# RWKV's triangular inverse: 32x32 block transposes on VectorE in place of the second update product on TensorE

## The chip, the cores and the metric

The kernel runs on one core of a Trainium2 chip. A core has five engines with a queue each: TensorE (PE, matmuls from SBUF into PSUM), VectorE (DVE), ScalarE (ACT), GpSimd (POOL) and SyncE (SP, which issues DMAs here). They meet through semaphores alone: an instruction that has to wait for a count holds everything behind it on its own engine. The metric is the device time of one execution in microseconds (us); lower is better.

## The reference

One inference step of a hybrid layer: sparse attention beside an RWKV-7 time mixing, then a gated sum, an output projection and an MLP. The change concerns the time mixing, whose recurrence is written step by step:

```python
def rwkv7_mix(p_rw, shift0, wkv0, p):
    ...
    def step(S, inp):
        r_t, d_t, k_t, v_t, kk_t, b_t = inp
        sa = jnp.einsum('bhij,bhj->bhi', S, kk_t)
        S = (S * d_t[:, :, None, :] - sa[..., None] * b_t[:, :, None, :]
             + v_t[..., None] * k_t[:, :, None, :])
        return S, jnp.einsum('bhij,bhj->bhi', S, r_t)

    S_T, ys = lax.scan(step, wkv0.astype(f32),
                       (tm(r_h), tm(decay), tm(k_h), tm(v_h), tm(kk), tm(b_h)))
```

There are 8 heads of 64 channels, a prompt of 512 tokens and 8 samples of 16 tokens.

## The kernel before

The 640 tokens are five tiles of 128, and each tile is two chunks of 64 tokens. The order is the samples' tile first (`TILE_AT`, tile 0 of the stage), then the four of the prompt. Inside a chunk the recurrence is solved at once: the products of the decayed keys give a strictly triangular 64x64 matrix per head, and the inverse of the identity minus it is needed. It is built by doubling. The 2x2 blocks are known directly, and each of the levels 0, 1, 2, ... merges neighbouring blocks to size 4, 8, 16, 32, 64 (`merges(i)`: 3 levels for the samples, whose chunks are 16 long, 5 for the prompt; level 4 is written out apart). So before the last level the matrix is block-diagonal with blocks of at most 32x32.

`invs[i % 2]` holds, for two groups of four heads (p = 0 and 1; the two chunks lie in the lower and upper 64 partitions), the inverse (index 0) and its transpose (index 1). One level is a ring through three engines, once for each p:

- `pe_part` (L999): 8 matmuls, the level's masked block matrix times the inverse, into PSUM;
- `act_part` (L1681): ScalarE copies the product to `part`;
- `pe_update`: 16 matmuls, alternately L1019 (transposed inverse and `part`, the update of the inverse) and L1021 (`part` and the transposed inverse, the update of its transpose); a tile's last level has L1021 alone;
- `dve_inverse` (L2228): VectorE adds both updates to `invs[:, p]` in one instruction of 128x512.

An fp32 matmul of this kind is two records in the trace, so 8 matmuls show as x16. The masked matrices (`merge`, L722) come from GpSimd.

The head of a tile: `pe_pairs` (L956) makes two sets of key products. VectorE masks the first into `br` (L2203), takes the 2x2 blocks from it (`dve_first`, L2210 and L2213, which give the transposed first level), for p = 0 and p = 1 in turn, and then masks the second set into `kr` (L2203 again). `pe_first` (L976) transposes the first level with the identity, 8 matmuls for each p, and `act_first` (L1672) copies the result to `invs[:, p, 0]`. Level 0's `pe_part` waits for that copy, for `kr` and for the mask.

The order on each engine is written out by hand. Tile 0 is prepared alone; then `pe_from_v(0)` (L939, a helper's line: small products of several kinds), the pairs of tile 1 and its levels, mixed with the samples' states; then a loop over i = 1, 2, 3, in which tile i's state steps (`pe_from_state`, `pe_u` L1058, `pe_to_state`, `pe_u_to_state`, `pe_outputs`, most of them L939; VectorE's `dve_state`, L2234 and L2236, after them) are set between the first levels of tile i + 1; then tile 4 alone. In the loop `pe_from_state(i, 1, 0)` follows `pe_first` and waits for the first `dve_state`, which stands behind `kr` in VectorE's queue. `pe_turn` (L967) transposes three operands of a tile on TensorE. After the stage come the attention steps, the branch products and the MLP, all dense.

Of the kernel before, what the change touches and what calls it, by code (L numbers as in the profile page):

```python
# [246 lines left out]
def merges(i):  # L247

    return 5 if i else 3
# [10 lines left out]


def g_sets(i):

    return 2 * i - 1 if i else 0
# [45 lines left out]
def build(nc, dram):  # L310
# [130 lines left out]
    with ExitStack() as ctx:  # L441
        def sem(name):
            return ctx.enter_context(nc.semaphore(name))
# [36 lines left out]
        pair_mm, pair_set, merge_set = [sem("pair_mm0"), sem("pair_mm1")], sem("pair_set"), sem("merge_set")  # L480
        inv_t_first, first_turned, inv_first = sem("inv_t_first"), sem("first_turned"), sem("inv_first")
        part_mm, part_set, update_mm, inv_set = sem("part_mm"), sem("part_set"), sem("update_mm"), sem("inv_set")
# [289 lines left out]
        def _(pe):  # L772
# [151 lines left out]
            def half(n):  # L924

                return slice(HD * n, HD * n + HD)
# [42 lines left out]

            def pe_first(i):  # L970

                for p in range(2):
                    pe.wait_ge(inv_t_first, 2 * i + p + 1)
                    for j in range(4):
                        for c in range(2):
                            done = mm(acc[half(c), p, 512 + j * HD:512 + (j + 1) * HD], invs[i % 2][half(c), p, 1, j, :],  # L976
                                      ident[half(c), half(c)], start=True, stop=True)
                    done.then_inc(first_turned, 1)

            def pe_part(i, level, p):  # L980
# [22 lines left out]
            def pe_update(i, level, p):  # L1003

                n, last = stage(i, level), level == merges(i) - 1
                pe.wait_ge(part_set, 2 * n + p + 1)
                inv, inv_t = invs[i % 2][:, p, 0], invs[i % 2][:, p, 1]
                if level == 4:
                    for j in range(4):
                        for c in range(2):  # L1010
                            at_ = 768 + j * HD + HB
                            done = mm(acc[first(c), p, at_:at_ + HB], part[second(c), 4 * p + j, 0:HB], inv_t[second(c), j, HB:HD],
                                      start=True, stop=True)
                    done.then_inc(update_mm, 1)
                    return
                for j in range(4):
                    for c in range(2):
                        if not last:
                            mm(acc[half(c), p, 512 + j * HD:512 + (j + 1) * HD], inv_t[half(c), j, :], part[half(c), 4 * p + j, :],  # L1019
                               start=True, stop=True)  # L1020
                        done = mm(acc[half(c), p, 768 + j * HD:768 + (j + 1) * HD], part[half(c), 4 * p + j, :],  # L1021
                                  inv_t[half(c), j, :], start=True, stop=True)
                done.then_inc(update_mm, 1)
# [111 lines left out]
            pe_turn(0, 0)  # L1135
            pe_first(0)
            for level in range(merges(0)):
# [28 lines left out]
            done.then_inc(u_mm, 1)  # L1166
            pe_first(1)
            pe.wait_ge(u_set, 1)
# [20 lines left out]
            for i in range(1, NT - 1):  # L1189
# [14 lines left out]
                pe_turn(following, 0)  # L1204
                pe_first(following)
                pe_from_state(i, 1, 0)
# [258 lines left out]
        def _(act):  # L1465
# [202 lines left out]

            def act_first(i):
                for p in range(2):  # L1670
                    act.wait_ge(first_turned, 2 * i + p + 1)
                    do(A(columns(invs[i % 2][:, p, 0]), acc[:, p, 512:768], ACT.Copy), inv_first)  # L1672

            def act_part(i, level):
# [34 lines left out]
            act_turned(0, 0)  # L1709
            act_first(0)  # L1710
            act_part(0, 0)
# [12 lines left out]
            act_u(0, every)  # L1724
            act_first(1)
            act_turned(1, 0)
# [11 lines left out]
            for i in range(1, NT - 1):  # L1738
# [3 lines left out]
                act_turned(following, 0)  # L1742
                act_first(following)
                act_g(i, upper)
# [243 lines left out]
        def _(dve):  # L1988
# [209 lines left out]
            def dve_pairs(i, n, p):  # L2198
# [6 lines left out]
                   pair_set)  # L2205

            def dve_first(i, p):

                first = invs[i % 2][:, p, 1]
                do(V.tensor_tensor(first, acc[:, p, 512:1024].rearrange("q (j a d) -> q j a d", j=4, a=2)[:, :, 0, :],  # L2210
                                   over_heads(e_masks[:, E_PAIRT:E_PAIRT + HD], 4), ALU.mult))
                do.settle()
                do(V.tensor_tensor(first, first, over_heads(e_masks[:, E_IDENT:E_IDENT + HD], 4), ALU.add), inv_t_first)  # L2213

            def dve_inverse(i, level, p):

                dve.wait_ge(update_mm, 2 * stage(i, level) + p + 1)
                if level == 4:
# [4 lines left out]
                    return  # L2223
                if level == merges(i) - 1:
                    dst, src = invs[i % 2][:, p, 1].rearrange("q j d -> q (j d)"), acc[:, p, 768:1024]
                else:
                    dst, src = invs[i % 2][:, p].rearrange("q n j d -> q (n j d)"), acc[:, p, 512:1024]
                do(V.tensor_tensor(dst, dst, src, ALU.add), inv_set)  # L2228

# [416 lines left out]
```

## Time and profile before

| | us |
|---|---|
| median of 3 runs | 1146.52 (1146.48 to 1149.2) |
| the profiled execution, own time | 1146.62 |
| its span, first to last instruction | 1144.8 |
| TensorE busy | 1104.5 |
| VectorE busy | 693.5 |
| GpSimd busy | 634.3 |
| ScalarE busy | 398.5 |
| mean granted clock of TensorE | 0.990 |

Busy time is the time in which an engine had an instruction under way; idle time of an engine that nobody waits for costs nothing. Times inside the trace are counted from the span's start. The granted clock is a share of TensorE's full 2.4 GHz.

### The profile page before, as it was taken

The numbers are of one execution on the slowest core, as the hardware profiler recorded it, in microseconds if no ns is written. First come the engines' busy times: TensorE is split into PE (matmuls) and PEld (weight loads), VectorE is DVE, ScalarE is ACT, GpSimd is POOL, SyncE is SP. The second block draws the span as 40 slices with busy tenths as digits, with TensorE's granted clock in tenths as the row PEclk, the third lists the DMA queues.
The fourth block names the chain that finished last, engine by engine and source line by source line (L and its number), as shares of the span: only waits on it lengthen the run. The fifth ranks groups of instructions, "written<-read, shape, count | busy, mean of one in ns | idle before, by whom it ended". The sixth has DMA issues, their size and how long they took to land.

```text
span 1144.8 us, 25249 instructions
## 1 busy us (share of the span) xinstructions
PE 1104.5 (96%) x10421; PEld 1042.0 (91%) x10421; DVE 693.5 (61%) x1172; ACT 398.5 (35%) x758; POOL 634.3 (55%) x687
## 2 busy tenths in 40 slices
PE   7999999989999999999999999999999999999996
PEld 6887989879888899887899999999999999999995
DVE  6863776773555378765344434676358647745787
ACT  5342333443333343333341122343134223413453
POOL 7932556551321047533236655678568857866783
PEclk9999999999999899999999999999999999999998
DMA  7343532220100232222232223222223133213122
GB/s 248 97 83 58 97 89 86 65 82 4 40 4 3 86 102 61 64 76 74 67 137 74 75 74 104 80 74 74 93 74 92 49 101 90 59 56 112 54 75 92
DMA packets 48343, 89.37 MB, mean 78 GB/s; under 512 B 6729, under 2 KB 11217, under 8 KB 48049
## 3 DMA queue, kind: packets, MB, share of 16 engines
q1 hardware_dynamic: 43568, 77.88, 22.3%
q10 hardware_dynamic: 4672, 10.04, 4.3%
q8 instruction: 76, 1.25, 0.4%
q14 instruction: 27, 0.21, 0.1%
HBM read 80.06 MB, written 7.83 MB: 77 GB/s over the span
## 4 chain that ended last, share of the span: by engine, by line
PE 73%; DVE 20%; ACT 4%; issue 2%; POOL 0%; DMA 0%; ACTq 0%; DVEq 0%; POOLq 0%
PE acc L786 17%; PE acc L787 11%; PE wk L1423 8%; PE acc L1423 7%; PE wk L786 6%; PE wk L787 4%; PE wk L939 3%; PE acc L1019 2%; DVE hid_lo L2435 1%; PE acc L1021 1%; PE acc L999 1%; DVE invs L2228 1%; PE acc L823 1%; PE acc L1278 1%; PE wk L1305 1%
## 5 line engine op out<-in xcount | busy, mean ns | idle before, releaser
L675 POOL TENSOR_TENSOR w_lo<-w_raw,w_hi 128x512 fp32r<-128x512 f32 x178 | 247.4, 1390 | 14.8
L672 POOL TENSOR_TENSOR w_hi<-w_raw,ones_w 128x32 fp32r<-128x32 f32 x178 | 59.8, 336 | 316.4 <-PE acc L787 257.6
L786 PE MATMUL acc<-h_hi,w_hi 128*128 128x384 f32 x424 | 151.1, 356 | 4.5 <-DVE h_lo L2040 2.0
L786 PE MATMUL acc<-h_lo,w_hi 128*128 128x384 f32 x424 | 144.2, 340 | 0.0
L786 PE MATMUL acc<-h_hi,w_lo 128*128 128x384 f32 x424 | 143.9, 339 | 0.0
L673 POOL TENSOR_SCALAR w_hi<-w_raw 128x480 fp32r<-128x480 f32 x178 | 120.0, 674 | 0.1
L787 PE MATMUL acc<-h_hi,w_hi 128*128 128x256 f32 x424 | 119.0, 281 | 0.0
L787 PE MATMUL acc<-h_lo,w_hi 128*128 128x256 f32 x424 | 119.0, 281 | 0.0
L787 PE MATMUL acc<-h_hi,w_lo 128*128 128x256 f32 x424 | 118.8, 280 | 0.0
L786 PEld LDWEIGHTS acc<-h_hi,w_hi 128*128 128x128 f32 x424 | 80.2, 189 | 13.6 <-issue 6.4
L750 POOL TENSOR_TENSOR p_lo<-w_sum,p_hi 128x512 fp32r<-128x512 f32 x44 | 64.9, 1478 | 29.5 <-ACT p_hi L1945 29.5
L787 PEld LDWEIGHTS acc<-h_hi,w_hi 128*128 128x128 f32 x424 | 80.3, 189 | 0.3
L787 PEld LDWEIGHTS acc<-h_lo,w_hi 128*128 128x128 f32 x424 | 80.3, 189 | 0.0
L786 PEld LDWEIGHTS acc<-h_lo,w_hi 128*128 128x128 f32 x424 | 80.3, 189 | 0.0
L786 PEld LDWEIGHTS acc<-h_hi,w_lo 128*128 128x128 f32 x424 | 80.2, 189 | 0.0
L787 PEld LDWEIGHTS acc<-h_hi,w_lo 128*128 128x128 f32 x424 | 80.2, 189 | 0.0
L1914 ACT ACTIVATE squares<-scaled 128x640 f32<-128x640 f32 x32 | 23.7, 741 | 128.7 <-DVE scaled L2442 128.7
L722 POOL TENSOR_TENSOR merge<-br,e_masks 128x512 f32<-128x512 f32 x19 | 24.8, 1317 | 60.6 <-PE acc L999 30.5
L2228 DVE TENSOR_TENSOR invs<-invs,acc 128x512 f32<-128x512 f32 (+1 forms) x38 | 25.5, 672 | 47.3 <-PE acc L1021 47.0
L2492 DVE TENSOR_TENSOR x<-x,wk 128x320 f32<-128x320 f32 x64 | 30.2, 484 | 26.7 <-PE wk L1423 26.1
L1423 PE MATMUL wk<-hid_hi,p_hi 128*128 128x320 f32 x144 | 44.8, 311 | 1.4 <-DVE scaled L2442 1.3
L2492 DVE TENSOR_TENSOR x<-x,acc 128x320 f32<-128x320 f32 x64 | 30.1, 483 | 25.8 <-PE acc L1423 25.6
(453 smaller groups left out, 3242.9 us busy)
## 6 DMA issues: line engine op xcount, KB each, us to landing
w_raw<-w SPq DMA_DIRECT2D x178, 256.0 KB, 2.6
w_block<-w SPq DMA_DIRECT2D x64, 256.0 KB, 3.0
line_scratch<-line ACTq DMA_DIRECT2D x8, 384.0 KB
xT<-xT SPq DMA_DIRECT2D x4, 640.0 KB, 6.6
x<-xT ACTq DMA_DIRECT2D x1, 2560.0 KB, 9.9
bias_p<-line_scratch SPq DMA_DIRECT2D x8, 256.0 KB, 4.6
kc<-k_cache SPq DMA_DIRECT2D x8, 256.0 KB, 2.7
vc<-v_cache SPq DMA_DIRECT2D x8, 256.0 KB, 2.7
```

The costliest lines, as they stand in the source:

```text
L672: nc.gpsimd.tensor_tensor(hi[:, s, 0:LEAD], w_raw[:, r, 0:LEAD], ones_w[:], ALU.mult).then_inc(w_high, 1)
L673: nc.gpsimd.tensor_scalar(hi[:, s, LEAD:], w_raw[:, r, LEAD:], 1.0, 1.0, ALU.mult, ALU.mult).then_inc(w_high, 1)
L675: nc.gpsimd.tensor_tensor(lo[:, s, :], w_raw[:, r, :], hi[:, s, :].bitcast(F32), ALU.subtract).then_inc(w_split, 1)
L722: nc.gpsimd.tensor_tensor(merge[n % 2][:], br[i % 2][:, :, 0, :], over_heads(m, NH), ALU.mult).then_inc(merge_set, 1)
L750: nc.gpsimd.tensor_tensor(lo, factor(FACTORS[k % PRODUCTS][0]), hi.bitcast(F32), ALU.subtract).then_inc(p_split, 1)
L786: mm(out[:, 0:CUT], w_, x_[:, k0 + b, 0:CUT], start=go, stop=end)
L787: done = mm(out[:, CUT:T], w_, x_[:, k0 + b, CUT:T], start=go, stop=end)
L939: return mm(out, lhsT, rhs, start=start, stop=True, skip_group_check=True)
L1423: done = mm(out, w_[:, b * P:(b + 1) * P], x_[:, b, x, :], start=first and b == 0 and m == 0, stop=b == PAIRS - 1 and m == 2, skip_group_c ...
L1914: A(squares[:, r, :], scaled[:, r, :], ACT.Square).then_inc(hid_sq, 1)
L2228: do(V.tensor_tensor(dst, dst, src, ALU.add), inv_set)
L2492: V.tensor_tensor(x, x, product_banks(quarter, g)[FACTORS[n][2]], op).then_inc(out_read, 1)
```

## The change

The first level and the updated inverse are transposed by VectorE, which transposes each 32x32 block of its operand where it stands. `pe_first` and `act_first` are gone: `dve_first` itself writes `invs[:, p, 0]`. `pe_update` keeps one product, that of the inverse (in the last level, that of the transpose), `dve_inverse` adds 128x256 elements in place of 128x512 and then transposes the sum into `invs[:, p, 1]`, and TensorE's next update waits for that (`inv_turned`). Level 4 stays, but for this wait.

```diff
+def turned_at(i, level, p):
+
+    return (4 * (2 * i - 1) if i else 0) + 2 * (level - 1) + p + 1
...
-            def pe_first(i):
-
-                for p in range(2):
-                    pe.wait_ge(inv_t_first, 2 * i + p + 1)
-                    for j in range(4):
-                        for c in range(2):
-                            done = mm(acc[half(c), p, 512 + j * HD:512 + (j + 1) * HD], invs[i % 2][half(c), p, 1, j, :],
-                                      ident[half(c), half(c)], start=True, stop=True)
-                    done.then_inc(first_turned, 1)
...
                 n, last = stage(i, level), level == merges(i) - 1
                 pe.wait_ge(part_set, 2 * n + p + 1)
+                if level:
+                    pe.wait_ge(inv_turned, turned_at(i, level, p))
...
-                        if not last:
-                            mm(acc[half(c), p, 512 + j * HD:512 + (j + 1) * HD], inv_t[half(c), j, :], part[half(c), 4 * p + j, :],
-                               start=True, stop=True)
-                        done = mm(acc[half(c), p, 768 + j * HD:768 + (j + 1) * HD], part[half(c), 4 * p + j, :],
-                                  inv_t[half(c), j, :], start=True, stop=True)
+                        out = acc[half(c), p, 512 + j * HD:512 + (j + 1) * HD]
+                        if last:
+                            done = mm(out, part[half(c), 4 * p + j, :], inv_t[half(c), j, :], start=True, stop=True)
+                        else:
+                            done = mm(out, inv_t[half(c), j, :], part[half(c), 4 * p + j, :], start=True, stop=True)
...
-                pe_first(following)
...
-            def act_first(i):
-                for p in range(2):
-                    act.wait_ge(first_turned, 2 * i + p + 1)
-                    do(A(columns(invs[i % 2][:, p, 0]), acc[:, p, 512:768], ACT.Copy), inv_first)
...
                 do(V.tensor_tensor(first, first, over_heads(e_masks[:, E_IDENT:E_IDENT + HD], 4), ALU.add), inv_t_first)
+                do.settle()
+                do(V.transpose(one_inverse(i, p, 0), one_inverse(i, p, 1)), inv_first)
...
-                if level == merges(i) - 1:
-                    dst, src = invs[i % 2][:, p, 1].rearrange("q j d -> q (j d)"), acc[:, p, 768:1024]
-                else:
-                    dst, src = invs[i % 2][:, p].rearrange("q n j d -> q (n j d)"), acc[:, p, 512:1024]
-                do(V.tensor_tensor(dst, dst, src, ALU.add), inv_set)
+                last = level == merges(i) - 1
+                dst = one_inverse(i, p, 1 if last else 0)
+                do(V.tensor_tensor(dst, dst, acc[:, p, 512:768], ALU.add), inv_set)
+                if not last:
+                    do.settle()
+                    do(V.transpose(one_inverse(i, p, 1), dst), inv_turned)
```

Two places show how it moves instructions; line numbers are each kernel's own. On TensorE, the head of tile 0 from the turn of its first operand (`vt`) on, before:

```order
L967 MATMUL wk<-const_75,vt 128x128 [waits bonus_set]
L967 MATMUL wk<-const_75,vt 128x128 x3
L976 MATMUL acc<-const_75,invs_114 64x64 [waits inv_t_first]
L976 MATMUL acc<-const_75,invs_114 64x64 x7
L976 MATMUL acc<-const_75,invs_114 64x64 [waits inv_t_first]
L976 MATMUL acc<-const_75,invs_114 64x64 x7
L999 MATMUL acc<-invs_114,merge_117 64x64 [waits merge_set,pair_set,inv_first]
L999 MATMUL acc<-invs_114,merge_117 64x64 x7
L999 MATMUL acc<-invs_114,merge_117 64x64 [waits merge_set,pair_set,inv_first]
L999 MATMUL acc<-invs_114,merge_117 64x64 x7
```

The same place on TensorE now, to the end of level 0's updates:

```order
L972 MATMUL wk<-const_75,vt 128x128 [waits bonus_set]
L972 MATMUL wk<-const_75,vt 128x128 x3
L994 MATMUL acc<-invs_114,merge_117 64x64 [waits merge_set,pair_set,inv_first]
L994 MATMUL acc<-invs_114,merge_117 64x64 x7
L994 MATMUL acc<-invs_114,merge_117 64x64 [waits merge_set,pair_set,inv_first]
L994 MATMUL acc<-invs_114,merge_117 64x64 x7
L972 MATMUL wk<-const_75,bt 128x128 [waits turn_set]
L972 MATMUL wk<-const_75,bt 128x128 x3
L1019 MATMUL acc<-part,invs_114 64x64 [waits part_set]
L1019 MATMUL acc<-part,invs_114 64x64 x7
L1019 MATMUL acc<-part,invs_114 64x64 [waits part_set]
L1019 MATMUL acc<-part,invs_114 64x64 x7
```

The part products (L999, now L994) stand right behind the turn, and each update is 8 matmuls of one kind.

On VectorE, the head of the first loop pass (tile 2 is prepared, `br_112` and `invs_114` are its buffers, tile 1's state steps run), before:

```order
L2203 TENSOR_TENSOR br_112<-acc,e_masks 128x512 [waits pair_mm0,y_mm]
L2210 TENSOR_TENSOR invs_114<-acc,e_masks 128x256
L2213 TENSOR_TENSOR invs_114<-invs_114,e_masks 128x256 [waits dve_own]
L2203 TENSOR_TENSOR br_112<-acc,e_masks 128x512 [waits pair_mm1]
L2210 TENSOR_TENSOR invs_114<-acc,e_masks 128x256
L2213 TENSOR_TENSOR invs_114<-invs_114,e_masks 128x256 [waits dve_own]
L2203 TENSOR_TENSOR kr<-acc,e_masks 128x512 [waits pair_mm0,fv_mm]
L2203 TENSOR_TENSOR kr<-acc,e_masks 128x512 [waits pair_mm1]
L2234 TENSOR_TENSOR state<-wk,state 128x256 [waits state_mm]
L2236 TENSOR_TENSOR state<-state,pc 128x256 [waits dve_own]
```

The same place on VectorE now:

```order
L2189 TENSOR_TENSOR br_112<-acc,e_masks 128x512 [waits pair_mm0,y_mm]
L2200 TENSOR_TENSOR invs_114<-acc,e_masks 128x256
L2203 TENSOR_TENSOR invs_114<-invs_114,e_masks 128x256 [waits dve_own]
L2205 STREAM_TRANSPOSE invs_114<-invs_114 128x256 [waits inv_t_first]
L2189 TENSOR_TENSOR br_112<-acc,e_masks 128x512 [waits pair_mm1]
L2200 TENSOR_TENSOR invs_114<-acc,e_masks 128x256
L2203 TENSOR_TENSOR invs_114<-invs_114,e_masks 128x256 [waits dve_own]
L2205 STREAM_TRANSPOSE invs_114<-invs_114 128x256 [waits inv_t_first]
L2189 TENSOR_TENSOR kr<-acc,e_masks 128x512 [waits pair_mm0,fv_mm]
L2189 TENSOR_TENSOR kr<-acc,e_masks 128x512 [waits pair_mm1]
L2227 TENSOR_TENSOR state<-wk,state 128x256 [waits state_mm]
L2229 TENSOR_TENSOR state<-state,pc 128x256 [waits dve_own]
```

Two transposes stand ahead of `kr` and of the state's two instructions.

## Rows read from the trace of the kernel before

**Rows 1.** The page, its first part: busy us, share of the span, instructions.

```profile
PE 1104.5 (96%) x10421; PEld 1042.0 (91%) x10421; DVE 693.5 (61%) x1172; ACT 398.5 (35%) x758; POOL 634.3 (55%) x687
```

**Rows 2.** Stretches of the stage: length, each engine's busy us (instructions), granted clock, DMA.

```profile
249.31:265.10 15.79, 15.29 (x458) 14.51 (x457) 4.11 (x7) 6.29 (x13) 1.73 (x2) 1.00 0.01 3
334.89:355.77 20.88, 19.67 (x574) 18.22 (x576) 9.47 (x20) 7.14 (x17) 3.30 (x3) 1.00 0.01 3
355.77:358.50 2.73, 2.73 (x99) 2.73 (x101) 0.57 (x2) 0.00 (x0) 0.29 (x1) 1.00 0.03 6
385.62:394.76 9.14, 7.84 (x178) 6.95 (x177) 1.42 (x4) 3.18 (x6) 0.29 (x1) 1.00 0.75 247
```

**Rows 3.** Four stretches of 5 us, the same columns (PE, PEld, DVE, ACT, POOL, clock).

```profile
245.00:250.00 5.00, 3.23 (x78) 2.58 (x72) 4.77 (x8) 1.36 (x3) 2.68 (x2) 1.00 0.65 213
390.00:395.00 5.00, 3.82 (x87) 3.41 (x86) 0.85 (x2) 2.83 (x5) 0.00 (x0) 0.99 0.87 291
395.00:400.00 5.00, 4.85 (x76) 4.69 (x76) 0.72 (x2) 0.92 (x2) 0.00 (x0) 0.50 0.10 25
400.00:405.00 5.00, 5.00 (x43) 4.66 (x40) 3.29 (x11) 1.90 (x2) 0.00 (x0) 0.50 0.41 131
```

**Rows 4.** Timeline, TensorE's state steps: start us, us, engine, line, operation, [idle before].

```profile
342.02 1.10 PE L939 MATMUL wk<-u_sb,br 64*64 64x64 f32 x32
...
389.77 1.08 PE L1058 MATMUL wk<-g_sb,invs 64*64 64x64 f32 x15
...
393.39 0.68 PE L939 MATMUL wk<-state,ar 64*64 64x64 f32 x16 [1.08 <-DVE state L2236]
...
394.76 1.57 PE L1058 MATMUL wk<-g_sb,invs 64*64 64x64 f32 x13
...
399.36 1.97 PE L939 MATMUL wk<-u_sb,br 64*64 64x64 f32 x32
```

**Rows 5.** Timeline, updates and parts: tile 0's last level, loop pass 2's late levels.

```profile
262.37 1.13 PE L1021 MATMUL acc<-invs,part 64*64 64x64 f32 x32
...
348.23 0.34 PE L1019 MATMUL acc<-part,invs 64*64 64x64 f32 x4
...
350.20 0.68 PE L999 MATMUL acc<-invs,merge 64*64 64x64 f32 x16
...
351.13 0.68 PE L999 MATMUL acc<-invs,merge 64*64 64x64 f32 x16 [0.25 <-DVE invs L2228]
...
354.51 0.34 PE L991 MATMUL acc<-invs,br 32*32 32x32 f32 x10 [0.41 <-DVE invs L2228]
```

**Rows 6.** Timeline, VectorE at the start of the stage.

```profile
244.45 0.27 DVE L2277 MEMSET state<- 128x256 f32 x1 [0.19 <-DVE bonus L2165]
```

**Rows 7.** Timeline, head of loop pass 2, several engines.

```profile
331.20 2.69 POOL L722 TENSOR_TENSOR merge<-br,e_masks 128x512 f32<-128x512 f32 x2 [4.94 <-DVE br L2203]
...
331.49 1.27 DVE L2213 TENSOR_TENSOR invs<-invs,e_masks 128x256 f32<-128x256 f32 x1
...
332.55 0.66 PE L967 MATMUL wk<-const,vt 128*128 128x128 f32 x4
332.68 1.27 DVE L2203 TENSOR_TENSOR kr<-acc,e_masks 128x512 f32<-128x512 f32 x2
...
334.32 0.43 DVE L2236 TENSOR_TENSOR state<-state,pc 128x256 f32<-128x256 f32 x1
...
334.89 0.51 PE L939 MATMUL wk<-state,ar 64*64 64x64 f32 x10 [0.61 <-DVE state L2236]
```

**Rows 8.** Instructions of line L2228: count, duration ns min/median/max, first and last start, forms.

```profile
L2228 DVE TENSOR_TENSOR invs<-invs,acc x38: 420/686/689, 252.4 to 383.6; 128x512 f32<-128x512 f32 x36, 128x256 f32<-128x256 f32 x2
```

**Rows 9.** Timeline, head of tile 0: the turn, kr, the parts.

```profile
245.59 0.66 PE L967 MATMUL wk<-const,vt 128*128 128x128 f32 x4
...
248.56 1.28 DVE L2203 TENSOR_TENSOR kr<-acc,e_masks 128x512 f32<-128x512 f32 x2
...
249.34 1.28 PE L999 MATMUL acc<-invs,merge 64*64 64x64 f32 x32
```

More of the change, by code:

```diff
@@ L480, in build @@
         pair_mm, pair_set, merge_set = [sem("pair_mm0"), sem("pair_mm1")], sem("pair_set"), sem("merge_set")
-        inv_t_first, first_turned, inv_first = sem("inv_t_first"), sem("first_turned"), sem("inv_first")
+        inv_t_first, inv_turned, inv_first = sem("inv_t_first"), sem("inv_turned"), sem("inv_first")
         part_mm, part_set, update_mm, inv_set = sem("part_mm"), sem("part_set"), sem("update_mm"), sem("inv_set")
@@ L1135, in _ @@
             pe_turn(0, 0)
-            pe_first(0)
             for level in range(merges(0)):
@@ L1166, in _ @@
             done.then_inc(u_mm, 1)
-            pe_first(1)
             pe.wait_ge(u_set, 1)
@@ L1709, in _ @@
             act_turned(0, 0)
-            act_first(0)
             act_part(0, 0)
@@ L1724, in _ @@
             act_u(0, every)
-            act_first(1)
             act_turned(1, 0)
@@ L1742, in _ @@
                 act_turned(following, 0)
-                act_first(following)
                 act_g(i, upper)
@@ L2205, in dve_pairs, with one_inverse @@
                    pair_set)
+            def one_inverse(i, p, n):
+                return invs[i % 2][:, p, n].rearrange("q j d -> q (j d)")
             def dve_first(i, p):
```

## The prediction

> **What bounds the kernel now.** I read the page first: TensorE is busy for 1104.5 of 1144.8 us [rows 1], so most of the kernel is a stream of dense matmuls that the change does not touch. Then the table by stages. The touched code is RWKV's chunk stage, from 244 to 401 us of the span: a tile 0, a tile 1, three passes of one loop and a last tile. The loop stretch from the wait for the state to the next tile has PE busy for 19.67 of 20.88 us, tile 0's for 15.29 of 15.79 [rows 2]. So this stage too is nearly bound by TensorE, with a ring through ScalarE and VectorE at each merge level. The same tables show a second thing. The granted clock is 1.00 (the 2.4 GHz level) throughout the stage except at its end. The stretch 390 to 395 us had PE busy for 3.82 of 5 us with one idle gap of 1.08 us [rows 3, 4], and behind it the clock was 0.50 (1.2 GHz) from 395 to 405 us, although PE was then busy for 4.85 and 5.00 of 5 us [rows 3]. There the engine ran 64-wide matmuls at half speed, and the clock rose only after the dense 128-wide products had begun.
>
> **The change: what leaves.** One update product of every level but a tile's last goes: 18 levels. In the loop both halves' updates take 350.20 - 348.23 = 1.97 us for 64 records [rows 5]. The 32 that stay are seen in tile 0's last level, which already does one product: 1.13 us [rows 5]. So each level frees TensorE of 0.84 us. The 16 matmuls per tile that transposed the first level go too, from a place where TensorE waits anyway. ScalarE loses two copies per tile, which nobody then waits for.
>
> **What comes.** 46 VectorE transposes of 128x256 fp32, 10 for the first level and 36 in the levels, each behind a wait on the addition ahead of it. No row shows one. From below it is bounded by the memset of as many elements, 0.27 us [rows 6]; from above by the first-level addition that stood beside a GpSimd operation, 1.27 us [rows 7]. I take 0.43, the state's multiplication of the same shape [rows 7], nearest because it also reads and writes SBUF one element at a time; with 0.04 for the wait, 0.47. By the Trainium skill ("VectorE: DVE Perf Modes", The three transpose paths) a 128x128 bf16 block transpose takes 311 ns, and by "Vector Engine (DVE) Microarchitecture Reference" (3.8) it streams one element per cycle per lane; my estimate from these two is 0.44 us, by which the sum below would be the same within 0.2 us; no run here shows it yet.
>
> **A level at full clock.** Before, part p1 of one level follows that of the last after 354.51 - 351.13 = 3.38 us [rows 5]: part, both updates, the 128x512 addition (0.69) [rows 8], part. Now the ring goes part p1, update p0, addition p0 (128x256: 0.42 [rows 8]), transpose p0, addition p1, since VectorE takes addition p1 behind transpose p0. That is 3.38 - 1.97 + 0.57 - 0.69 + 0.42 + 0.47 + 0.42 = 2.60, a gain of 0.78 per level. TensorE's new wait for the transposed inverse costs nothing: between addition p1 and the next update p1 stand part p1 (0.68) and ScalarE's copy, over 0.9 us against 0.47; a transpose longer than that would stand on the path.
>
> **The head of a tile.** Here the transposes lie in VectorE's queue ahead of the second mask product (kr) and of the state. In tile 0, part p0 starts when kr p0 is done (248.56 start, part at 249.34) [rows 9]; in the loop TensorE waits for the state's multiplication (334.32 + 0.43) before it goes on at 334.89 [rows 7]. Two transposes shift both by 2 x 0.47 = 0.94 us. GpSimd's first merges, which start behind the second br, shift by 0.47; level 0 needs the first of them more than a microsecond later, so that is hidden. No DMA moves. The matmuls that filled TensorE's wait are gone, so the wait becomes bare: in the loop from 333.21 (end of the turn) to 335.83, 2.6 us; in tile 0 from 246.25 to 250.28, 4.0 us. Before, the loop's gap was 0.61 us [rows 7], and tile 0's was broken up by the first-level products.
>
> **What the bare waits do.** The gap that stood before the fall at 395 was 1.08 us [rows 4]; the stretch 245 to 250, with PE idle for 1.77 of 5 us in pieces, kept 1.00 [rows 3]. Four bare waits of 4.0 and 2.6 us are well beyond both, and what follows each is the kind of 64-wide work during which the clock stayed at 0.50 from 395 on. So I forecast that the clock falls at each, and comes back only with the dense pair products of the next tile (128 columns, all four quadrants). The price of half clock, from the same work at both levels: outputs 1.97 against 1.10 us, a factor 1.79; the product with the inverse 1.57 / 13 against 1.08 / 15 per record, 1.68 [rows 4]. I take 1.75 on TensorE's busy time, and let it swallow the small waits.
>
> **The sum.**
> - Tile 0: (15.29 - 2 x 0.84) x 1.75 = 23.8, against 15.79: +8.0; shift +0.9; the pairs behind it at half clock +0.8 (an estimate from their share of the 2.73 us row): +9.7.
> - Tile 1 has no bare wait (TensorE is occupied while VectorE transposes): 4 x 0.78 = -3.1.
> - Loop passes 1 and 2: (19.67 - 4 x 0.84) x 1.75 = 28.5, against 20.88: +7.7; shift +0.9; from_v and pairs 2.73 x 0.75 = +2.0: +10.6 each, +21.3.
> - Pass 3: +7.7 + 0.9, and the last tile, which has no pairs, 7.84 x 1.75 - 9.14 = +4.6 [rows 2]: +13.2.
>
> Together +41.1. The profiled execution took 1146.62 us around a span of 1144.8, which agrees with the median of 1146.52; so 1187.7, I say **1188 us**.
>
> **The rivals.**
> 1. *The clock never falls.* For it: 245 to 250 kept 1.00. Against: its idle pieces were shorter. Then the full-clock terms count: tile 0 0.94 - 2 x 0.78 = -0.6; tile 1 -3.1; each pass 0.94 - 3.1 = -2.2: -10.3 in all, **1136.3**, faster. Beside it stands the Trainium skill's rule ("VectorE: DVE Perf Modes", Rules for kernel authors) that a 32x32 transpose is fastest on VectorE; taken by itself it says this outcome, and the trace has no row on it.
> 2. *The clock falls only in tile 0*, whose wait is longest: 9.7 - 3.1 - 6.6 = 0, **1146.6**, no change. Short falls at every wait, about 2.5 us each, come out at the same.
> 3. *It falls in tile 0 and in some passes*, or rises half-way through a pass: each pass that is slow costs 10.6 + 2.2 = 12.8 more, so **1150 to 1180**. For it: at half clock nothing in the trace shows the dense update levels, only the last tile's mix. It is slower all the same.
> 4. *Transposes at 1.27 us at full clock* (held up by GpSimd as the first-level addition is): shift 2 x 1.31 = 2.6 four times, and the ring 2.60 + 0.84 = 3.44 against 3.38: about +12, **1158**. By these terms the time is that of before at a transpose of 0.83 us (26 us more per microsecond of it: eight in the heads, one in each of 18 levels), and slower beyond. Against it: the two kr products, with one operand in SBUF, ran beside the second of these GpSimd operations in 1.27 us for both [rows 7], no slower than elsewhere, and a transpose too has one.
>
> That the transposes don't replace the products is excluded by the order of instructions.
>
> **How the numbers follow.** 0.3% is 3.4 us, about what a measurement of this kernel tells from no change. Forecast 0.50; rival 3 0.23; rival 2 0.12; rival 1 0.10; rival 4 0.05. Slower: 0.50 + 0.23 + 0.05 = 0.78; same 0.12; faster 0.10. The range: below, it leaves out most of rival 1 and begins at 1139; above, tile 1 at half clock would cost about what a pass does, 7.7 in place of -3.1, and the factor 1.79 another 3, so 1202. The forecast's own range is 1172 to 1202.
>
> **What would show it.** Right: a group of 46 transposes near 0.43 us; the update group with half its records; an idle of about 4 us before the first part of tile 0 and 2.6 us before from_state in each pass, released by VectorE; a granted clock of 0.50 from about 251 to 266 us and in the later part of each pass, with part and update records at nearly twice their length; tile 1's levels shorter at 1.00. Wrong: a clock of 1.00 across the stage (then rival 1 holds), half clock over only a few microseconds (rival 2), or transposes above a microsecond (rival 4).

## The result, and the profile after

The changed kernel takes 1139.07 us (median; single executions from 1136.12 to 1145.98) against 1146.66 us, a ratio of 0.9946 with a 95% interval of 0.9931 to 0.9961. It is faster by 7.6 us, a little beyond the 0.3% that can be told from no change; the forecast was 41 us slower. Measured a second time, on chip 13, it was 3.1 us faster (0.9962 to 0.9993, under "Both kernels again"), so what is sure is the sign and a few microseconds. Its profiled execution took 1137.34 us around a span of 1135.6 us. All times in this document leave out two slow executions, one of 1336 us (the changed kernel, measured again) and one of 2228 us (the filled waits, measured again), and the trace of the second, the only one of that run, is not used.

The page of the changed kernel, its first part and the start of the chain that ended last (answers to [rows 1]):

```profile
PE 1083.1 (95%) x9677; PEld 1020.5 (90%) x9685; DVE 702.3 (62%) x1218; ACT 395.0 (35%) x748; POOL 634.5 (56%) x687
...
PE 70%; DVE 21%; issue 4%; ACT 3%; POOL 1%; DMA 0%; ACTq 0%; DVEq 0%; POOLq 0%
```

TensorE lost 21.4 us of busy time, VectorE gained 8.8: 46 transposes at 0.445 us are 20.5, less the narrower additions. Groups of VectorE in the stage (240 to 395 us): line, operation, count | busy us, mean ns | idle before:

```profile
L2221 DVE STREAM_TRANSPOSE invs<-invs 128x256 f32<-128x256 f32 x36 | 16.0, 446 | 1.2
L2218 DVE TENSOR_TENSOR invs<-invs,acc 128x256 f32<-128x256 f32 x38 | 15.6, 410 | 31.9 <-PE acc L1019 27.4 <-PE acc L1017 4.5
...
L2205 DVE STREAM_TRANSPOSE invs<-invs 128x256 f32<-128x256 f32 x10 | 4.5, 445 | 0.3
```

The bare waits of TensorE are there as forecast, 4.0 us in tile 0 and 2.3 to 2.9 us in the loop passes. From TensorE's timeline: start us, us, line, operation, [idle before and who ended it]; compare [rows 7, 9]. The first row names GpSimd's merge, but this part needs only the first of two merges, which ended at 250.23. What it also needs, the `kr` product of half p0, ended on VectorE at 251.56, 0.10 us before the part began, so VectorE ended this wait as it did the others:

```profile
251.66 1.98 PE L994 MATMUL acc<-invs,merge 64*64 64x64 f32 x32 [4.01 <-POOL merge L727]
...
307.00 0.51 PE L944 MATMUL wk<-state,ar 64*64 64x64 f32 x10 [2.59 <-DVE state L2229]
...
334.28 0.51 PE L944 MATMUL wk<-state,ar 64*64 64x64 f32 x10 [2.34 <-DVE state L2229]
...
361.91 0.53 PE L944 MATMUL wk<-state,ar 64*64 64x64 f32 x11 [2.94 <-DVE state L2229]
```

What is not there is the half clock that should have followed them. Stretches of 5 us (PE, PEld, DVE, ACT, POOL busy, granted clock, DMA), behind the wait of tile 0, at the end of tile 1, and around the waits of two passes:

```profile
250.00:255.00 5.00, 3.34 (x43) 2.92 (x44) 2.12 (x4) 1.04 (x3) 2.90 (x3) 0.60 0.08 26
255.00:260.00 5.00, 4.94 (x102) 4.57 (x102) 2.25 (x6) 1.69 (x4) 0.00 (x0) 0.72 0.00 0
...
295.00:300.00 5.00, 5.00 (x134) 4.94 (x135) 1.74 (x5) 0.60 (x1) 5.00 (x5) 0.66 0.33 109
...
305.00:310.00 5.00, 3.00 (x89) 3.03 (x91) 1.82 (x4) 1.73 (x5) 1.81 (x2) 1.00 0.01 3
...
330.00:335.00 5.00, 2.66 (x78) 2.39 (x74) 4.03 (x8) 1.18 (x3) 2.68 (x2) 1.00 0.00 0
```

In tile 0 the clock fell, to the 1.2 GHz level, from about 251.0 to 257.8 us, and was back at 2.4 GHz while TensorE still ran 64-wide parts and updates. Behind the waits of the passes, with PE busy for as little as 2.66 of 5 us, it stayed at 1.00. It also fell for 3.4 us at the end of tile 1. Such a stretch at half clock is called a fall below. The fall of 10 us at the end of the stage [rows 3] is not in this trace.

All that follows compares the steps of the stage. A step runs from one tile's first state products (`wk<-vt,kr`) to the next tile's; tile 0's begins with its first pair product, the last ends with the first attention logit. Lengths in us, from the starts in TensorE's timeline; in brackets the length of a fall, from stretches of 1 us. Two falls in the last column run on behind the stage. The falls in pass 1 of after, the filled waits, behind, and behind and filled, and those in the passes and the last tile of the transposes twice, do not follow a wait in that step: they begin at the step's border, from 0.7 us ahead of it to 0.5 us into it:

| trace | tile 0 | tile 1 | pass 1 | pass 2 | pass 3 | last | sum |
|---|---|---|---|---|---|---|---|
| before | 19.65 | 32.67 | 29.90 | 29.80 | 29.85 | 15.71 (6.4 of 10.2) | 157.58 |
| before, second trace | 20.86 (3.4) | 32.66 | 29.89 | 29.79 | 29.80 | 12.97 | 155.97 |
| after | 20.75 (6.8) | 29.89 | 28.66 (3.4) | 27.28 | 27.63 | 12.98 | 147.19 |
| after, second trace | 20.40 (6.8) | 29.77 | 30.94 (10.2) | 30.75 (10.2) | 30.93 (10.2) | 12.98 | 155.77 |
| levels only | 17.81 | 29.94 | 26.54 | 26.37 | 26.37 | 12.98 | 140.01 |
| head only | 22.69 (6.8) | 32.49 | 33.76 (6.8) | 33.79 (6.8) | 30.70 | 12.98 | 166.41 |
| filled waits | 19.57 (3.4) | 29.76 | 28.86 (3.4) | 27.27 | 27.63 | 12.98 | 146.07 |
| long waits | 19.69 (3.4) | 29.76 | 31.04 (6.8) | 30.83 (6.8) | 30.77 (6.8) | 12.98 | 155.07 |
| transposes behind | 20.42 (6.8) | 29.92 | 27.71 (3.4) | 27.90 (3.4) | 30.18 (10.2) | 15.69 (6.3 of 10.2) | 151.82 |
| behind and filled | 18.72 | 29.76 | 27.96 (3.4) | 26.37 | 26.73 | 12.97 | 142.51 |
| transposes twice | 21.28 (6.8) | 32.05 | 30.84 (3.4) | 30.78 (3.4) | 30.76 (3.4) | 14.19 (3.4) | 159.90 |
| levels, late | 18.52 (3.4) | 29.54 | 26.37 | 26.19 | 26.23 | 12.97 | 139.82 |

Between the two first traces of before and after the stage gave 10.4 us, of which 2.7 is the fall that before had in its last tile. The stage began 1.4 us later after (245.09 against 243.68 at the first pair product; in the dense work ahead of it that trace has a second fall of 3.4 us, at 90 us), and the spans differ by 9.2.

### The profile page after: what moved, and what is told of

It reads as the page before. It is cut to its first block, busy times and chain, and to the rows that moved or that the text cites. A ratio compares the mean times of both kernels' runs of the same rounds, so it can differ in the third digit from the quotient of the medians.

```text
span 1135.6 us, 23841 instructions
## 1 busy us (share of the span) xinstructions
PE 1083.1 (95%) x9677; PEld 1020.5 (90%) x9685; DVE 702.3 (62%) x1218; ACT 395.0 (35%) x748; POOL 634.5 (56%) x687
## 4 chain that ended last, share of the span: by engine, by line
PE 70%; DVE 21%; issue 4%; ACT 3%; POOL 1%; DMA 0%; ACTq 0%; DVEq 0%; POOLq 0%
PE acc L791 17%; PE acc L792 11%; PE wk L1417 8%; PE acc L1417 7%; PE wk L791 6%; PE wk L792 4%; PE wk L944 2%; DVE hid_lo L2428 1%; PE acc L994 1%; PE acc L828 1%; PE acc L1019 1%; PE wk L1299 1%; DVE invs L2218 1%; DVE xT L2021 1%; PE acc L1272 1%
## 5 line engine op out<-in xcount | busy, mean ns | idle before, releaser
L680 POOL TENSOR_TENSOR w_lo<-w_raw,w_hi 128x512 fp32r<-128x512 f32 x178 | 247.8, 1392 | 14.8
L1417 PE MATMUL acc<-hid_hi,p_hi 128*128 128x320 f32 x144 | 44.7, 310 | 0.2
```

The costliest lines, as they stand in the source:

```text
L680: nc.gpsimd.tensor_tensor(lo[:, s, :], w_raw[:, r, :], hi[:, s, :].bitcast(F32), ALU.subtract).then_inc(w_split, 1)
L1417: done = mm(out, w_[:, b * P:(b + 1) * P], x_[:, b, x, :], start=first and b == 0 and m == 0, stop=b == PAIRS - 1 and m == 2, skip_group_c ...
```

## The experiments

The theory after the result (A): the terms of the sum that were reckoned at full clock are right, and the clock falls only for some microseconds. The forecast's own reason (B): each bare wait costs the clock until the next tile's dense products. The runs were made on three chips, each beside the kernel before, to which its ratio is taken: the levels alone, the head alone, the filled waits and the longer waits on chip 8; the transposes behind, twice and late, and the changed kernel again, on chip 13; the others on chip 2.

**The levels alone.** `pe_first` and `act_first` stay as before; the levels are the changed kernel's.

```diff
+            pe_first(0)
...
+            act_first(0)
...
-                do.settle()
-                do(V.transpose(one_inverse(i, p, 0), one_inverse(i, p, 1)), inv_first)
```

> The transposes of the levels are kept; the head of a tile is that of the kernel before (TensorE transposes the first level, ScalarE copies it). Theory A (the terms at full clock hold, the clock falls only for some microseconds and mostly at the long bare wait of tile 0): 18 levels x 0.78 = 14.0 us less than before, about 1132.5, and some 6 us less than the changed kernel (4 shifts of 0.94 and a fall in tile 0 of 2 to 3 us are gone). Theory B (the forecast: every bare wait costs the clock until the next tile's dense products): no bare wait is left, so 1132.5 too. Rival C (the levels gain less, because a ring of VectorE and ScalarE bounds them): 18 x 0.4 = 7 us less, 1139, the same as the changed kernel.

1130.69 us (1127.89 to 1133.6), ratio 0.9866, interval 0.9846 to 0.9887: 15.5 us faster than before, and faster than the change itself. A and B both forecast this; C falls. The steps at full clock give the size of a level: tile 0 (19.65 - 17.81) / 2 = 0.92, tile 1 (32.67 - 29.94) / 4 = 0.68, passes (29.85 - 26.43) / 4 = 0.86 us.

**The head alone.** The first level by VectorE, both update products as before.

```diff
-                            done = mm(out, inv_t[half(c), j, :], part[half(c), 4 * p + j, :], start=True, stop=True)
+                            mm(acc[half(c), p, 512 + j * HD:512 + (j + 1) * HD], inv_t[half(c), j, :], part[half(c), 4 * p + j, :],
+                               start=True, stop=True)
...
+                    dst, src = invs[i % 2][:, p].rearrange("q n j d -> q (n j d)"), acc[:, p, 512:1024]
```

> Only the first level is transposed by VectorE; the levels are those of the kernel before, with both update products. Theory A: 4 shifts of 0.94 and a fall in tile 0 of 2 to 3 us: +6 us against before, about 1152.5. Theory B: half clock from each of four bare waits to the next tile's dense products: tile 0 15.79 x 0.75 = +11.8, three passes 20.88 x 0.75 = +15.7 each, less the waits it swallows, about +50, 1195. Rival C (the heads cost nothing, all of the change is in the levels): 1146.5.

1151.45 us, ratio 1.0044 (1.0028 to 1.006): 5.3 us slower than before, what A said, and a tenth of B's 50. Of the whole change, then, the levels give and the head takes. Pass 3 kept the clock through a wait of 2.59 us and is 30.70 long, 0.85 more than before: that is the shift alone. Passes 1 and 2, with 6.8 us at half clock, are 3.1 longer.

**The bare waits filled.** The changed kernel, with the first-level matmuls left in TensorE's queue; nothing reads their result.

```diff
             pe_turn(0, 0)
+            pe_first(0)
...
                 pe_turn(following, 0)
+                pe_first(following)
```

> The changed kernel with the first-level matmuls left in TensorE's queue (8 for each p, behind the turn, in tile 0 and in the loop); nothing reads their result. They end before the state or kr is there, so the path is the same and only the bare waits are broken up: tile 0's 4.0 us into pieces of 2 us and less, the passes' 2.3 to 2.9 us to about 1.3. Theory A: the clock keeps 1.00 in tile 0, about 2 us less than the changed kernel, 1137, and its runs lie closer together. Theory B: the same sign, 1136. Rival C (the falls have nothing to do with the bare waits): 1139, as the changed kernel, with a fall still at 251 us.

1135.76 us (1131.39 to 1138.46), ratio 0.9895 (0.9874 to 0.9917), and once more on chip 2:

> The changed kernel with the idle first-level matmuls left in TensorE's queue, once more, for a second trace and its time on the chip of this call. Theory A: no falls longer than 4 us in the passes, 1134 to 1137. Rival C (the filler had luck in its first trace): falls of 7 to 10 us in the passes as in the second trace of the changed kernel, 1142.

1135.6 us (1134.2 to 1136.0), ratio 0.9904 (0.9883 to 0.9924). Matmuls whose result nobody uses make the kernel faster: both intervals lie below that of the change (0.9931 to 0.9961). In the trace of the first run the waits in the passes are 1.5 to 1.9 us, and no pass lost its clock at one:

```profile
330.00:335.00 5.00, 3.49 (x94) 3.15 (x90) 3.15 (x6) 1.49 (x3) 1.91 (x2) 1.00 0.00 0
```

In tile 0 the wait was split (2.06 us was its longest piece) and the clock still fell, but for 3.4 us in place of 6.8; there A said more than came. The falls of the second run can't be read in a trace, but the mean granted clock of its six executions (0.991 to 0.994) lies with the executions of the changed kernel that lose no clock in the passes (0.984 to 0.991) and not with those that do (0.978 to 0.982; both groups under "Both kernels again"), which speaks against its rival C.

**Longer bare waits.** Three more transposes ahead of `kr` in each loop pass.

```diff
+                for again in range(3):
+                    do.settle()
+                    do(V.transpose(one_inverse(following, 1, 0), one_inverse(following, 1, 1)))
                 dve.wait_ge(fv_mm, i + 1)
```

> The changed kernel with three more VectorE transposes (the same result again) ahead of kr in each of the three loop passes: TensorE's bare wait there grows from 2.3 to 2.9 us to about 3.8, near tile 0's 4.0. Shift alone: 3 x 1.45 = +4.4, 1143.5. Theory A: the clock falls as in tile 0 and comes back after 3 to 7 us of 64-wide work: +2 to 3 us more in each pass, 1150 to 1153. Theory B: half clock up to the next tile's dense products, some 20 us at a factor of 1.75: +8 us more in each pass, about 1168. Rival C (the length of the wait is not what drops the clock): 1143.5.

1144.39 us (1142.26 to 1146.95), ratio 0.9981 (0.997 to 0.9992). All three waits, now 4.0 to 4.2 us, were followed by half clock, as B says; but each for 6.8 us only. TensorE in pass 2, then two stretches of it and the one behind:

```profile
335.84 0.80 PE L944 MATMUL wk<-state,ar 64*64 64x64 f32 x10 [4.03 <-DVE state L2229]
```

```profile
335.00:340.00 5.00, 4.16 (x65) 4.19 (x67) 0.66 (x2) 1.36 (x3) 1.25 (x1) 0.50 0.01 3
340.00:345.00 5.00, 4.31 (x134) 4.17 (x133) 2.37 (x6) 1.24 (x3) 0.24 (x2) 0.94 0.01 3
```

The pass is 30.83 us, 3.55 more than the 27.28 of the changed kernel: 1.45 for the three transposes and 2.1 for the clock, where B has 8. So A's price of a pass came, but its total of 1150 to 1153 was 6 us too much, and that the median lies by C's 1143.5 is chance, since the falls are there. The traces show where most of A's excess comes from: it was added to a kernel that has falls of its own, which cost 2.0 us in tile 0 and 1.4 at the start of pass 1 in after's first trace, where this trace has 1.0 and none.

**The transposes behind kr and the state.** The same ten transposes at another place in VectorE's queue.

```diff
             for p in range(2):
                 dve_pairs(0, 1, p)
+                dve_turn_first(0, p)
...
                 dve_state(i, 0)
+                for p in range(2):
+                    dve_turn_first(following, p)
```

> The changed kernel with the first level's transposes moved: in tile 0 each stands behind its kr product, in the loop both stand behind the first multiplication of the state. Theory A (a head costs what stands ahead of kr and of the state on VectorE, not the transposes as such): three passes 0.9 us shorter each, tile 0 0.45, so -3.2 against the changed kernel, and the passes' bare wait shrinks to about 1.6 us, so that fewer of them drop the clock: 1133 to 1136. Rival C (the two transposes cost the same wherever they stand, since part p0 waits for the first of them): 1139. Rival D (TensorE's matmuls in the head were worth their time as a filler for the clock; a bare wait of 1.6 us drops it as well): 1136 with falls still in the passes.

1135.13 us, but from 1128.15 to 1142.44; ratio 0.993 (0.9895 to 0.9965). The pass without its falls is that of the levels alone (see the next run), so the 0.9 us of a head is its place in the queue. Tile 0 gained nothing: part p1 now waits for the transpose that stands last (a row of it under the next run). A wait of only 1.7 to 2.0 us was followed by half clock in two passes of three, which is what D said. Pass 3, the wait and ten records at half speed (0.51 us where the clock is full):

```profile
359.40 0.80 PE L944 MATMUL wk<-state,ar 64*64 64x64 f32 x10 [2.03 <-DVE state L2232]
```

**The same with the waits filled.**

> The first level's transposes behind kr and the state, as in the run that moved them (1135, from 1128 to 1142), and beside that the first-level matmuls left in TensorE's queue, with nothing reading their result. Theory A (the path is now that of the run that kept only the levels, and the matmuls fill the bare waits): the clock keeps 1.00 in the passes, 1130 to 1132, with its runs within some 6 us. Rival C (the filler makes no difference to the clock): 1135, spread over 14 us as without it.

1132.14 us (1129.9 to 1135.75), ratio 0.9879 (0.9854 to 0.9905): 3 us less and a spread of 6 in place of 14. The two intervals overlap, and the chips differ, so the 3 us alone does not show the filler's worth. The clock says more: no execution here has a mean granted clock under 0.988, where three of the seven without the filler have 0.978 to 0.980, and the trace has no fall at a wait of the passes, where the other has two. Pass 2 is 26.37, to the hundredth that of the levels alone. Parts p0 and p1 of tile 0's first level, each behind its transpose:

```profile
250.20 0.68 PE L1003 MATMUL acc<-invs,merge 64*64 64x64 f32 x16 [0.40 <-DVE invs L2219]
251.25 0.68 PE L1003 MATMUL acc<-invs,merge 64*64 64x64 f32 x16 [0.37 <-DVE invs L2219]
```

This pair of runs tells the two costs of the head apart: the path is that of the run before, and only the unused matmuls differ.

**The transposes of the levels twice.**

```diff
+                    do(V.transpose(one_inverse(i, p, 1), dst))
+                    do.settle()
                     do(V.transpose(one_inverse(i, p, 1), dst), inv_turned)
```

> The changed kernel with each of the 36 transposes of the levels made twice (same result). Theory A (VectorE's addition, transpose, addition is the ring that sets a level, so one transpose of a level stands on the path): 18 x 0.47 = +8.5, about 1147.5. Rival C (a level is now set by TensorE's parts and updates, 2.3 of 2.4 to 2.6 us, and the transposes lie beside them): up to 1141, at most +2. A price between would say that some levels are bound by the one and some by the other.

1152.22 us (1145.71 to 1162.7), ratio 1.0078 (1.0046 to 1.0111), 9.6 more than the changed kernel on the same chip; A forecast 8.5. Its executions spread over 17 us, with mean granted clocks from 0.967 to 0.988, so falls are mixed into the 9.6, and the steps say more. Tile 1, without a fall, is 32.05 against 29.8: 0.56 for each of four levels. So one transpose in each level stands on the path. The two parts of a late level on TensorE; p1 waits for its addition, which VectorE takes behind both transposes of p0:

```profile
350.56 0.68 PE L994 MATMUL acc<-invs,merge 64*64 64x64 f32 x16
351.83 0.68 PE L994 MATMUL acc<-invs,merge 64*64 64x64 f32 x16 [0.58 <-DVE invs L2218]
```

**Both transposes behind both additions,** with the head of before.

```diff
-                if not last:
-                    do.settle()
-                    do(V.transpose(one_inverse(i, p, 1), dst), inv_turned)
+                if not last and not (i, level, p) in held:
+                    dve_turned(i, p)
+                if not last and (i, level, p - 1) in held:
+                    dve_turned(i, 0)
+                    dve_turned(i, 1)
```

> Head of the kernel before, levels of the changed one, as in the run that kept only the levels (1130.7), but where the additions of both halves follow each other on VectorE (tile 0, two levels of tile 1, three levels of each loop pass) both transposes stand behind both additions, so that addition p1 no longer waits for transpose p0. Theory A (addition p1 stood on the ring behind transpose p0): a level falls from 2.4 to 2.6 us to TensorE's own 2.35, 13 levels x 0.2 = -2.6, about 1128. Rival C (the levels are set by TensorE already): 1130.7. Rival E (the later transpose p0 makes the next update wait): slower, 1133 and more.

1127.98 us (1126.04 to 1130.19), ratio 0.9863 (0.9836 to 0.989). It beats both kernels, but against the levels alone (0.9866, on another chip) nothing can be told from the total, and that it meets A's 1128 is no proof of A: by the steps it gains 0.14 to 0.18 us a pass and 0.40 in tile 1, about 0.9 where A forecast 2.6. The parts of both halves now follow each other in 1.15 us, but the level takes 341.97 - 339.45 = 2.52 us, where the levels alone take 339.99 - 337.42 = 2.57 (second pair of rows); TensorE's own part and update, 1.15 each, are 2.3 of either, so C is nearer the truth than A:

```profile
339.45 1.15 PE L1004 MATMUL acc<-invs,merge 64*64 64x64 f32 x32
...
341.97 0.77 PE L996 MATMUL acc<-invs,br 32*32 32x32 f32 x32 [0.21 <-DVE invs L2240]
```

```profile
337.42 1.47 PE L1004 MATMUL acc<-invs,merge 64*64 64x64 f32 x32
...
339.99 0.44 PE L996 MATMUL acc<-invs,br 32*32 32x32 f32 x16
```

**Both kernels again.**

> The changed kernel once more, for its time beside the others of this call and for a second trace. Both theories: 1139, between 1136 and 1146 from one execution to the next. Theory A: a fall of 3 to 7 us in tile 0 in every trace, and falls in some of the passes in one trace that are not there in another, each costing 1 to 3 us; that is what spreads its times. Rival C (the spread comes from the dense stages): the passes have the same lengths in both traces.

1142.62 us (1139.4 to 1145.3), ratio 0.9978 (0.9962 to 0.9993): the same kernel on chip 13, and hardly faster than before. The interval does not meet that of the first measurement (0.9931 to 0.9961): each tells what its executions scatter by, and not how the kernel differs from one measurement to the next. Its second trace shows what differs. The waits are the same (2.75, 2.33 and 2.94 us), and this time each pass lost its clock. Pass 2: the wait, a part behind it, the next level's part, amid which the clock came back, and the stretches:

```profile
335.41 0.80 PE L944 MATMUL wk<-state,ar 64*64 64x64 f32 x10 [2.33 <-DVE state L2229]
...
336.29 1.96 PE L994 MATMUL acc<-invs,merge 64*64 64x64 f32 x29
...
343.96 1.67 PE L994 MATMUL acc<-invs,merge 64*64 64x64 f32 x29
```

```profile
330.00:335.00 5.00, 3.08 (x71) 2.78 (x68) 4.86 (x10) 1.19 (x2) 2.69 (x2) 0.99 0.01 3
335.00:340.00 5.00, 4.59 (x73) 4.62 (x75) 0.27 (x1) 1.37 (x4) 1.27 (x1) 0.50 0.01 3
340.00:345.00 5.00, 5.00 (x98) 5.00 (x95) 2.35 (x6) 0.58 (x1) 0.00 (x0) 0.50 0.01 3
345.00:350.00 5.00, 5.00 (x111) 4.29 (x110) 3.32 (x8) 2.38 (x5) 1.27 (x1) 0.98 0.00 0
```

Half clock for 10.2 us, and back at about 345, while the engine ran the 64-wide parts and products between two levels. The price is 30.75 - 27.28 = 3.5 us a pass. The profiled executions took 1145.32 and 1137.34 us, 8.0 apart; the three passes make 9.05 of that, the other steps give 0.5 back. Of the 20 executions of the first measurement 11 lie between 1136.1 and 1139.1 us and 9 between 1141 and 1146; of the second's eleven, ten lie above 1140. That the upper group are those that lose the clock in the passes is read from two traces, one of each group, and the mean granted clock of every execution bears it out: 0.984 to 0.991 in the 11 and 0.978 to 0.981 in the 9, 0.978 to 0.982 in the ten and 0.986 in the one. Why the second has so many more is open; the chip may have a part in it.

> The kernel before once more, for a second trace. Theory A: the same lengths of tile 0, tile 1 and the passes (19.65, 32.7, 29.8 us); the fall of 10 us at the last tile is a matter of the execution, like the other kernels' falls, and need not come again; 1141 to 1149.

1144.83 us. The same steps, no fall in the last tile behind the same wait of 1.09 us, and one of 3.4 us in tile 0 that the first trace did not have.

## Why the prediction was wrong, step by step

- **What leaves and comes.** Right. One update product of a level went; the transposes take 0.445 us where 0.43 was taken. All 46 lie within 445 to 447 ns, also those that run beside GpSimd's merges, so rival 4 falls. The first-level addition beside them is held up as before (1.32 us here, where its fellow of half p0 takes 0.43 without GpSimd):

```profile
248.96 2.67 POOL L727 TENSOR_TENSOR merge<-br,e_masks 128x512 f32<-128x512 f32 x2 [2.88 <-DVE br L2189]
...
249.18 1.32 DVE L2203 TENSOR_TENSOR invs<-invs,e_masks 128x256 f32<-128x256 f32 x1
250.54 0.45 DVE L2205 STREAM_TRANSPOSE invs<-invs 128x256 f32<-128x256 f32 x1
```

  By the Trainium skill ("GPSIMD Engine Reference", 1. Specifications) GpSimd contends with VectorE instructions that have two SBUF inputs; the trace agrees, since the addition has two and the transpose one.
- **A level at full clock.** Right: a late level of pass 2 takes 349.80 - 347.23 = 2.57 us from part p0 to part p0, where 2.60 was reckoned; before, the same stretch took 353.66 - 350.20 = 3.46 ([rows 5] and the row set apart below). The level ahead of it is shorter, 2.37. What sets the level is less sure than the size: with both transposes behind both additions it still took 2.52, so TensorE's own 2.3 us lie close under the ring that was reckoned. Over all, the run with the levels alone gives 14.8 us for 18 levels against 14.0. TensorE's parts and updates of these levels:

```profile
344.86 1.15 PE L994 MATMUL acc<-invs,merge 64*64 64x64 f32 x32
346.03 1.15 PE L1019 MATMUL acc<-part,invs 64*64 64x64 f32 x32
347.23 1.47 PE L994 MATMUL acc<-invs,merge 64*64 64x64 f32 x32
348.54 1.33 PE L1019 MATMUL acc<-part,invs 64*64 64x64 f32 x32
349.80 0.44 PE L986 MATMUL acc<-invs,br 32*32 32x32 f32 x16
```

```profile
353.66 0.44 PE L991 MATMUL acc<-invs,br 32*32 32x32 f32 x16
```

- **The head.** Right: a shift of 0.90 us in a pass (27.27 with filled waits against 26.37 for the levels alone), 0.94 forecast. The bare waits came, 4.01 and 2.34 to 2.94 us for 4.0 and 2.6.
- **What the bare waits do.** This step failed: "the clock falls at each, and comes back only with the dense pair products of the next tile". That it falls at each is true of some executions (all three passes of after's second trace) and not of others (none of the three in the first). That it comes back only with the dense products is wrong in every trace that has such a fall: the falls of the stage lasted 3.4 to 10.2 us (eleven of the twelve traces have some, that of the levels alone none), and behind a bare wait the clock rose amid 64-wide parts, updates and state steps. The fall in [rows 3] was 10 us long too, and ended where dense products had begun; the prediction took what stood beside the end for its cause. No row of before showed a return without dense products, and none showed that there is no such return.
- **The size.** The factor of 1.75 held: 29 records of a part at half clock take 1.96 us (after's second trace, above), 1.10 at full (before, a row below). It was applied to 16.3 us of TensorE's work in each pass; what ran at half clock was 3 to 10 us of the time behind the wait, or none. Measured against the step without a fall, one costs 0.9 to 1.2 us (3.4 long) or 1.7 to 2.0 (6.8 long) in tile 0, where 9.7 + 0.6 = 10.3 was reckoned, and in a pass 1.5 (3.4 long), 2.1 to 3.1 (6.8 long) or 3.3 to 3.6 (10.2 long), where 12.8 was.

```profile
336.49 1.10 PE L999 MATMUL acc<-invs,merge 64*64 64x64 f32 x29
```

- **The sum.** At full clock the steps after are 18.7, 29.8, 27.3, 27.3, 27.6 and 13.0 (tile 0's is from the run behind and filled, taken to have gained nothing there; pass 1, which has a fall in both traces, is taken to be like pass 2), in all 143.7, against 154.8 before (the steps of its first trace, the last tile at 12.97): -11.1, where rival 1 had -10.3. Between that and the -7.6 of the medians stand falls: after's in tile 0, 1.7 to 2.0 us in both traces, and those in the passes in some executions. Before has its own, 2.7 us in the last tile in one trace and 1.2 in tile 0 in the other. In the first trace of after that is -11.1 + 2.0 (tile 0) + 1.4 (pass 1) - 2.7 (before's) = -10.4, the stage's difference, which it meets by construction, since each price is a difference of these steps. So the outcome is rival 1 with such short falls as rival 2 counts, to which the prediction gave 0.22 together.
- **The range** began at 1139, to leave most of rival 1 out; the result stands at its very edge.

## What to carry to other kernels

A loss of clock is priced as an event with a length read from traces, not as a state that lasts until the work looks different; one fall in one trace gives neither its length nor its chance. When a product is taken off an engine that waits there anyway, the work may still have been worth its place: leaving unused matmuls in the wait made this kernel 3 us faster (from 1139.1 to 1135.8 and 1135.6). And a change made of two parts is to be costed and run as two: the levels alone give 15.5 us, twice the whole, since the head puts two transposes ahead of what TensorE waits for and gains nothing.

## What the runs showed of the hardware

Waits of TensorE of 3.5 to 4.2 us were followed by half clock in all of nine cases; waits of 2.3 to 2.9 us in 5 of 12, with the same kernel on both sides; waits of 1.5 to 2.1 us in 5 of 12 (in tile 0 of before's second trace, of the filled waits and of the late levels, and in two passes with the transposes behind); the wait of 1.1 us in the last tile in 2 of 12, one of them the fall in [rows 3]. The clock also fell without such a wait, for 3.4 us at the end of tile 1, behind a wait of 0.94 us and 32-wide products, in four of the eight traces that have this wait (after, 295.4 to 298.8):

```profile
294.03 0.44 PE L986 MATMUL acc<-invs,br 32*32 32x32 f32 x16 [0.94 <-DVE invs L2218]
...
295.73 3.40 PE L944 MATMUL wk<-vt,kr 64*64 64x64 f32 x62
```

The state products took 3.40 us there and 2.02 in the next pass. So a longer wait was followed by half clock more often, but below 3.5 us its length alone did not tell. What decides between two executions of one kernel whether a wait costs the clock stays open.
